# One 512-column matmul for the high weights: a change to the feed-forward loops of an fp32 block kernel on Trainium2

## What is computed

```python
# first block, layers 0 and 1 (conv0, conv1)
up = depthwise_conv(h @ ffn_w_up[l], ffn_conv_w[l], ffn_conv_b[l])     # three taps over the tokens
f = (jax.nn.silu(up[..., :D_FF]) * up[..., D_FF:]) @ ffn_w_down[l]
h = layer_norm(DEEPNORM_ALPHA * h + f, ln_ffn_g[l], ln_ffn_b[l])

# second block, twice per layer (ffn1.0, ffn2.0, ffn1.1, ffn2.1)
def swiglu(h, wi, wo):
    gate, up = jnp.split(h @ wi, 2, axis=-1)
    return (jax.nn.silu(gate) * up) @ wo
x = x + FFN_RESIDUAL * swiglu(rms_norm_2(x, ffn1_norm[i]), ffn1_wi[i], ffn1_wo[i])
```

## Time and profile before

| | |
|---|---|
| median of 3 runs | 1837.57 us (1837.57 to 1838.91) |
| span of the profiled execution, first to last instruction | 1835.9 us |
| busy: PE, PEld | 1797.0 us (98%), 1646.0 us (90%) |
| busy: DVE, ACT, POOL | 1242.9 us (68%), 898.3 us (49%), 94.9 us (5%) |
| mean granted clock of TensorE | 0.999 |
| matmuls | 12420 |

### The profile page before, as it was taken

The page is one execution under the profiler, slowest core; times in us unless marked ns, Lnnn a source line. Parts: engine busy times, 40 slices in busy tenths (PEclk is TensorE's granted clock), DMA queues, the critical chain, the costliest instruction groups (busy, mean ns, idle before and its releaser), DMA issues.

```text
span 1835.9 us, 31204 instructions
## 1 busy us (share of the span) xinstructions
PE 1797.0 (98%) x12420; PEld 1646.0 (90%) x12433; DVE 1242.9 (68%) x1557; ACT 898.3 (49%) x1093; POOL 94.9 (5%) x88
## 2 busy tenths in 40 slices
PE   6999999999999999999999999999999999999999
PEld 6977999897899989999988989999999987889998
DVE  6889876798977686555776655555655577556555
ACT  5566544446644444334645454333533367654332
POOL 1001200000300000000070000000000000000000
PEclk9999999999999999999999999999999999999999
DMA  9525755453574537554633635555555541425553
GB/s 326 182 93 177 260 173 194 160 159 104 179 258 173 206 122 240 185 186 154 189 115 124 243 115 170 190 189 183 174 186 186 192 144 59 172 92 188 187 188 123
DMA packets 232259, 318.55 MB, mean 174 GB/s; under 512 B 12150, under 2 KB 202518, under 8 KB 231670
## 3 DMA queue, kind: packets, MB, share of 16 engines
q1 hardware_dynamic: 226598, 295.97, 48.4%
q0 software_dynamic: 5296, 19.83, 3.4%
q10 hardware_dynamic: 288, 1.69, 0.2%
HBM read 313.27 MB, written 4.19 MB: 173 GB/s over the span
## 4 chain that ended last, share of the span: by engine, by line
PE 91%; DVE 4%; ACT 3%; issue 1%; DMA 0%; ACTq 0%; DVEq 0%
PE bank L708 49%; PE bank L983 19%; PE bank L876 7%; PE bank L731 4%; PE bank L717 3%; PE bank L765 1%; ACT w_hi L1610 1%; DVE w_lo L2242 1%; PE bank L1025 1%; PE bank L1049 1%; DVE x L2239 1%; PE bank L1168 0%; DVE bn L2342 0%; PE bank L1350 0%; PE bank L1364 0%
## 5 line engine op out<-in xcount | busy, mean ns | idle before, releaser
L2242 DVE TENSOR_TENSOR w_lo<-raw,w_hi 128x2048 fp32r<-128x2048 f32 (+2 forms) x279 | 641.6, 2308 | 302.5 <-ACT w_hi L1610 302.0
L1610 ACT ACTIVATE w_hi<-raw 128x2048 fp32r<-128x2048 f32 (+1 forms) x278 | 528.8, 1904 | 633.1 <-PE bank L708 407.9
L708 PE MATMUL bank<-xt_hi,w_hi 128*128 128x256 f32 x2552 | 724.5, 284 | 2.4 <-ACT rb L1610 2.4
L708 PE MATMUL bank<-xt_lo,w_hi 128*128 128x256 f32 x2552 | 722.0, 283 | 0.0
L708 PE MATMUL bank<-xt_hi,w_lo 128*128 128x256 f32 x2552 | 722.0, 283 | 0.0
L708 PEld LDWEIGHTS bank<-xt_hi,w_hi 128*128 128x128 f32 x2552 | 488.3, 191 | 6.6 <-issue 4.0
L708 PEld LDWEIGHTS bank<-xt_lo,w_hi 128*128 128x128 f32 x2552 | 488.3, 191 | 2.6 <-issue 0.2
L708 PEld LDWEIGHTS bank<-xt_hi,w_lo 128*128 128x128 f32 x2552 | 488.3, 191 | 0.2
L983 PE MATMUL bank<-w_hi,act_hi 128*128 128x512 f32 x528 | 206.5, 391 | 0.0
L983 PE MATMUL bank<-w_lo,act_hi 128*128 128x512 f32 x528 | 206.2, 390 | 0.0
L983 PE MATMUL bank<-w_hi,act_lo 128*128 128x512 f32 x528 | 205.4, 389 | 0.0
(11 more groups left out here) (339 smaller groups left out, 1951.9 us busy)
## 6 DMA issues: line engine op xcount, KB each, us to landing
raw<-in_ffn_wi SPq DMA_DIRECT2D x88, 1024.0 KB, 5.1
raw<-in_ffn_w_up SPq DMA_DIRECT2D x44, 1024.0 KB, 5.1
raw<-in_ffn_wo SPq DMA_DIRECT2D x44, 1024.0 KB, 4.9
raw<-in_ffn_w_down SPq DMA_DIRECT2D x22, 1024.0 KB, 5.4
raw<-in_w_in SPq DMA_DIRECT2D x14, 1024.0 KB, 5.6
raw<-in_ssd_in_proj SPq DMA_DIRECT2D x14, 1024.0 KB, 5.3
raw<-in_w_out SPq DMA_DIRECT2D x8, 1024.0 KB, 4.9
raw<-in_even_out_proj SPq DMA_DIRECT2D x8, 1024.0 KB, 5.0
```

The source lines that it names most:

```text
L708: ins = first(mm(dst, w[s][:, k, c0:c0 + m], xt[v][:, k, :], start=k == 0 and p == 0, stop=k == KT - 1 and p == 2))
L1610: return act.activation(dst, src, ACT.Copy)
L2242: return dve.tensor_tensor(out=out, in0=in0, in1=in1, op=op)
```

## The change

The high and low halves of the stream are laid side by side: `xt_both[P, KT, 2, T]`, with `xt_hi` and `xt_lo` as views of it. In the loops of all six feed-forward parts a new helper `tile_halves` makes one output tile into a bank of its own: per slice one 256-column matmul, low weights by high stream, into the left half of the bank, and one 512-column matmul, high weights by both streams, into the whole bank. The left half then holds high by high plus low by high, the right half high by low. Chunks 0 and the down projections are as before.

ScalarE copies the right half of each bank to SBUF (`copy_halves`, into `f_low`); VectorE adds it to the left half (`add_halves`), which frees the bank. Gate takes banks 0 and 1, up banks 2 and 3, in every chunk. Scaling, taps and the product read the sums in SBUF; the taps read `f_sum`.

In the convolution loop the order on both engines is another: the split of a weight unit stands between the sum of gate and its taps, and the split of the third unit stands ahead of the center and taps of up, where it stood behind the operand.

```diff
-        xt_hi = sb("xt_hi", [P, KT, T], F32R)
-        xt_lo = sb("xt_lo", [P, KT, T], F32R)
+        xt_both = sb("xt_both", [P, KT, 2, T], F32R)
+        xt_hi, xt_lo = xt_both[:, :, 0, :], xt_both[:, :, 1, :]
...
+        f_low = carve("ffn", 2, 2, T, at=FFN_TOP)
+        f_sum = carve("ffn", 2, 2, T, at=FFN_TOP + 1024)
...
+                def tile_halves(b, w, j, first):
+
+                    for k in range(KT):
+                        first(mm(bank[b][:, 0:T], w[1][:, k, P * j:P * j + P], xt_hi[:, k, :], start=k == 0, stop=False,
+                                 skip_group_check=True))
+                        ins = mm(bank[b][:, :], w[0][:, k, P * j:P * j + P],
+                                 xt_both[:, k, :, :].rearrange("p v t -> p (v t)"), start=False,
+                                 stop=k == KT - 1, skip_group_check=True)
+                    ins.then_inc(bank_full[b], 1)
...
-                        for b, kk in ((c % 2, k), (2 + c % 2, k + 1)):
-                            pe.wait_ge(bank_drained[b], base[b] + i)
-                            up_pair(kk, b, i)
+                        for b0, kk in ((0, k), (2, k + 1)):
+                            w, first = split_unit(kk, i, KT), First()
+                            for j in range(2):
+                                pe.wait_ge(bank_drained[b0 + j], i * 2 + base[b0 + j] + c - 1)
+                                tile_halves(b0 + j, w, j, first)
...
+            def copy_halves(tag, what, c, turn):
+
+                for j in range(2):
+                    b, n = names.of[f"{tag}.{what}{c}.{j}"]
+                    act.wait_ge(bank_full[b], turn * 2 + n)
+                    copy(f_low[:, "gu".index(what), j, :], bank[b][:, T:2 * T]).then_inc(half_copied, 1)
...
                 with act.Fori(0, TURNS, 1) as i:
+                    seen.enter(i, [(halves_summed, 4), (gate_scaled, 2)])
                     for c in (1, 2):
                         split_in_loop(tag, 3 * c + 1, i)
+                        copy_halves(tag, "g", c, i)
                         split_in_loop(tag, 3 * c + 2, i)
-                        chunk(c, i)
+                        sum_center(c, "g", f_gate, 0, i)
+                        copy_halves(tag, "u", c, i)
+                        split_in_loop(tag, 3 * c + 3, i)
+                        sum_center(c, "u", f_up, 22, i)
+                        act.wait_ge(gate_scaled, seen.next(gate_scaled))
+                        silu(c)
...
+            def add_halves(tag, dst, what, c, turn):
+
+                for j in range(2):
+                    b, n = names.of[f"{tag}.{what}{c}.{j}"]
+                    dve.wait_ge(half_copied, seen.next(half_copied))
+                    ins = tt_(dst[:, j, :], bank[b][:, 0:T], f_low[:, "gu".index(what), j, :], ALU.add)
+                    ins.then_inc(bank_drained[b], 1)
...
                     for c in (1, 2):
                         split_in_loop(tag, 3 * c + 1, i)
+                        sums(c, "g", i)
                         split_in_loop(tag, 3 * c + 2, i)
-                        chunk(c, i)
+                        taps(c, f_sum[:, 0, :, :], f_gate, 0, i).then_inc(gate_scaled, 1)
+                        sums(c, "u", i)
+                        split_in_loop(tag, 3 * c + 3, i)
+                        step(taps(c, f_sum[:, 1, :, :], f_up, 22, i))
+                        product(c)
```

More of the change, by code:

```diff
@@ L1802, in center, with sum_center, silu @@
                         at = bass.ds(44 + t, 1) if turn is None else bass.ds(turn * 4 + 44 + t, 1)
-                        ins = act.activation(dst[:, c % 2, j, :], bank[b][:, T * j:T * j + T], ACT.Identity,
+                        ins = act.activation(dst[:, c % 2, j, :], src[:, j, :], ACT.Identity,
                                              scale=par[:, cw, at], bias=par[:, cb, at])
                     ins.then_inc(center_ready, 1)
[L1807 to L1814, removed]
+                def sum_center(c, what, dst, tile0, turn):
+                    act.wait_ge(halves_summed, seen.next(halves_summed))
+                    center(c, f_sum[:, "gu".index(what), :, :], dst, tile0, turn)
+                def silu(c):
                     act.activation(f_silu[:, c % 2, :], f_gate[:, c % 2, :, :], ACT.Silu).then_inc(silu_ready, 1)
@@ L2535, in ffn @@
                 taken(f"{tag}.rb")
-                gate(0, None)
-                chunk(0, None)
+                first_gate()
+                first_product()
                 with dve.Fori(0, TURNS, 1) as i:
-                    seen.enter(i, [(vec_step, 2), (silu_ready, 2)])
+                    seen.enter(i, [(vec_step, 4), (silu_ready, 2), (half_copied, 8)])
                     for c in (1, 2):
@@ L2562, in taps, with sums, product @@
                             part = dst[:, c % 2, j, 1:T] if side == 0 else dst[:, c % 2, j, 0:T - 1]
-                            src = bank[b][:, T * j:T * j + T - 1] if side == 0 else bank[b][:, T * j + 1:T * j + T]
-                            ins = stt(part, src, w, part, ALU.mult, ALU.add)
+                            ins = stt(part, src[:, j, 0:T - 1] if side == 0 else src[:, j, 1:T], w, part, ALU.mult,
+                                      ALU.add)
                         if side == 0:
                             step(ins)
-                    ins.then_inc(bank_drained[b], 1)
-                def chunk(c, turn):
-                    taps(c, f"{tag}.g{c}", f_gate, 0, turn)
-                    taps(c, f"{tag}.u{c}", f_up, 22, turn)
-                    b, n = names.of[f"{tag}.u{c}"]
-                    dve.wait_ge(bank_drained[b], n if turn is None else turn + n)
+                    return ins
+                def sums(c, what, turn):
+                    add_halves(tag, f_sum[:, "gu".index(what), :, :], what, c, turn)
+                    halves_added(tag, what, c, turn)
+                    dve.sem_inc(halves_summed, 1)
+                def product(c):
                     dve.wait_ge(silu_ready, seen.next(silu_ready))
```

83 lines of the change are left out of this document (52 added, 31 removed).

## The result

The changed kernel takes **1844.6 us** in the median of four runs (1843.45 to 1847.85), the kernel before 1837.6 us. The ratio is 1.0039 with a 95% interval of 1.0027 to 1.005: the change makes the kernel slower by about 7 us. The forecast was 1830.4 us, and the range ended at 1841. It was wrong in sign.

The account below looks back on a forecast made before the run. TensorE's instruction spacing was taken to bound the loops, VectorE and ScalarE mattering only at loop ends. Merge -22.8, entries +9.6, exits +6.0 gave -7.2 us: forecast 1830.4 us, range 1823 to 1841, against 1837.57 before.

Parts of the forecast that it names:

- Term 1, the merge: Up-projection matmuls in the loops: each of 1920 merges saves 11.9 ns, -22.8 us, between -15.6 and -25.6.
- The lower bound of 8.1 ns: Smallest saving per merge in the loops, if every wide matmul took 231.7 ns like the first six: -15.6 us.
- The forecast's own signs: Trace signs against the forecast: a TensorE wait inside a steady chunk, narrow matmuls at 213 ns, or wide ones over 232 ns.
- the first rival: Loop matmuls: the merge saves 0, so the kernel takes 1853 us; decides if wide ones exceed 231.9 ns; chance 0.11.
- the 1848 us by it: Whole-kernel time if a merge in the loops saves only the skill page's 2.5 ns, -4.8 us in all.
- What ScalarE and VectorE get inside a loop: Copies and additions per convolution chunk: ScalarE 9.7, VectorE 14.8 of 16.6 us; both fit, nothing charged.
- The rival of a late VectorE: Convolution loops: hand-over waits exceed VectorE's 1.8 us to spare; at 1 us too much +12, 1842 us; chance 0.07.
- Term 2, entries: Loop entries: TensorE waits for bank 0 to be emptied by VectorE, +9.6 us, bounds +7 and +11.
- Term 3, exits: Two convolution loop exits: the last down unit waits for its operand, 3.0 us each, +6.0 us, between +5 and +7.
- The clock: New gaps in ffn1.0 and at two exits drop TensorE to 1.2 GHz, 1.4 us each, +4.3: 1834.7 us; chance 0.10.
- the added 15.6 us: Forecast cost at the loop ends: entries +9.6 us and convolution exits +6.0 us.
- The fixed 12 ns does not go: Loop matmuls: the width-independent 12 ns stays, the merge saves 0, +15.6 us, 1853 us; chance 0.11.

Follow-up runs that it names:

- 1: Changed kernel with eight wide matmuls, then eight narrow ones per tile, in place of one and one: 1836.4 us, ratio 0.999.
- 6: Changed kernel with two wide and two narrow matmuls in turn: 1835.6 us, ratio 0.9985.
- 7: Changed kernel with eight wide then eight narrow, loop banks exchanged within a pair, and third split behind the operand: 1824.9 us, ratio 0.9924.
- 10: Changed kernel with two wide and two narrow in turn, loop banks exchanged within a pair, and third split behind the operand: 1824.8 us, ratio 0.9922.
- 12: Changed kernel with runs of sixteen of a kind and exchanged banks, the third split left ahead of the taps: 1820.8 us, ratio 0.9911.
- experiment 2: Changed kernel without its merge, three 256-column matmuls per slice again, all else kept: 1857.9 us, ratio 1.0108.
- 8: Changed kernel with runs of sixteen (second tile narrow first), exchanged banks and third split behind the operand: 1822.6 us, ratio 0.9918.
- Experiment 3: Changed kernel with the two banks of each pair exchanged in the loops: 1834.6 us, ratio 0.9978.
- 9: Changed kernel with the wide matmul ahead of its narrow one, still one and one: 1848.2 us, ratio 1.0052.
- 11: Changed kernel with the narrow matmul adding into the right half of the bank: 1845.0 us, ratio 1.0041.
- 13: Changed kernel with the narrow matmul working four slices ahead: 1844.3 us, ratio 1.0038.
- 14: Changed kernel with the narrow matmul taking the high weights too, so the low by high pass is left out: 1847.2 us, ratio 1.0044.

## Why the prediction was wrong

**Term 1, the merge: this step failed.** It took the mean spacing of two pure series, 119.9 and 227.9 ns, for an alternation that no row showed, and got 11.9 ns for a merge. In strict alternation a pair takes 353.1 ns, so a merge brings 359.7 - 353.1 = 6.6 ns; 1920 of them are -12.7 us in place of -22.8. Down then starts slower (5.49 for 5.47), which leaves the -11.4 of the chunks. The lower bound of 8.1 ns failed too: it took the first six wide ones of the earlier trace rows, 231.7 ns, for the worst that a wide one behind narrow ones can be; each of them but one stood behind another wide one. The two switches in the earlier trace rows were read as free at a resolution of 10 ns, where the size in dispute was 4 ns in each wide one. Experiments 1, 6, 7, 10 and 12 show that the forecast's number was right for the instructions (347.8 to 348.3 ns) and wrong only for their order. The forecast's own signs said the same: the wide ones exceed 232 ns, and also the 231.9 at which the first rival decides. Of the 13.7 us between the forecast -7.2 and the measured +6.5 of the span, this term is 11.4, the clock 2.9, and entries and exits give back 0.6.

On the Trainium skill (TensorE: Matmul & The Clock Gate, "Back-to-back issue gap"): its isolated spacing of 215.8 ns for 512 columns was met in no series here; the lowest is 226. Its saving of 2.5 ns per merge is further from the measured 6.6 than my lower bound was. That the 1848 us by it lie closer to 1844.6 than my 1830.4 do is in part luck: its term 1 is -4.8 where the chunks gave -11.4, and the clock, which it left out as well, took back not quite half of that difference.

**What ScalarE and VectorE get inside a loop: right.** VectorE 14.7 us forecast as 14.8, ScalarE 9.6 as 9.7, no wait inside, and experiment 2 gives a chunk of 16.98 to the digit. The rival of a late VectorE did not come true in the changed kernel. It did in a small way where the matmuls were grouped, the banks exchanged and the split stood last (experiments 7, 8 and 10); with the split ahead of the taps it was gone (12).

**Term 2, entries: right in place and in size.** By the starts +9.2 us against +9.6: ffn1.0 +2.65 (forecast 2.7), the other three +0.65 each (0.7), the convolution entries +2.3 each (2.4 and 2.3). Experiment 3 shows that the exchange of two bank numbers buys it all back.

**Term 3, exits: right.** 2.9 us each, forecast 3.0.

**The clock: a rival that came in on top.** It had a chance of 0.10 as a case of its own, but it is a consequence of terms 2 and 3, not another case than the forecast: whoever expects gaps of 3 us should have put their clock price into the sum. Two of the three expected gaps were followed by a stretch at 1.2 GHz in the profiled run, at 1.4 and 1.5 us (expected 1.4 each), and filling the gaps gave back 3.9 us. Which gaps are followed changes from run to run, and the shorter ones of the convolution entries count too (last section). That fits the 1 to 4 us between kernels with the same chunks and the same waits (9, 11, 13 and 14).

**The fixed 12 ns does not go:** half true. It said that a saving of 8.1 ns breaks even with the added 15.6 us; the saving was 6.6, and the slower start of down and the clock made the rest. It was given 0.11 and priced as all or nothing; the truth lay between it and the forecast, where I had put no weight.

What stays open: why single narrow and wide matmuls in turn cost 5 ns a pair. Excluded are the order in the pair (9), the bank's half (11), the slice of the stream (13), the weight array (14) and a fixed price per change of width (6). Whether the weight loads or the matmuls themselves hold the pace was not separated by any run. The alternation by single instructions is left, as a fact without a mechanism.

## What to carry to other kernels

A spacing read in a pure series is not the spacing in a mixture: when the forecast hangs on a few ns per instruction, demand a row with the same order, or give the sign no better than even odds. Where matmuls of two widths are mixed, try them in groups of two or more; here, with 256 and 512 columns of fp32, that gave 8 to 9 us. At a loop's entry, look which bank the first tile takes; where an added 3 us gap on TensorE was followed by the lower clock, it cost about half as much again here. Read gaps from start to start, since a list of waits depends on which records are there.

## What the runs showed of the hardware

**Single alternation.** 353.1 ns a pair of 256 and 512 columns in turn, 348.3 ns in groups of two or eight, 347.8 in groups of sixteen; the narrow one takes 117 ns in single alternation, 115 in groups of two and 119 in groups of eight; the wide one 236, 233 (in groups of two), 230 (in groups of eight) or 226 when settled.

**The clock behind short gaps.** In the profiled runs of the changed kernel and its variants, a stretch at a granted clock of 0.50 stands behind every wait of 3.2 us at the entry of ffn1.0 that was left empty (nine of nine), behind 13 of 20 waits of 2.9 us at the convolution exits, and behind 8 of 20 waits of 2.0 us at the convolution entries.

**VectorE and GpSimd take turns.** The slow split of the earlier trace rows, which set the size of the convolution entries, has its cause in the trace of the changed kernel at conv0 (start us, us, engine, line, operation):

```profile
181.28 2.41 POOL L3202 TENSOR_TENSOR x<-mix,wide 128x1024 f32<-128x1024 f32 x1 [24.64 <-DVE w_lo L2277]
...
181.81 4.03 DVE L2277 TENSOR_TENSOR w_lo<-raw,w_hi 128x2048 fp32r<-128x2048 f32 x1 [0.70 <-ACT w_hi L1628]
...
183.77 4.28 POOL L3203 TENSOR_TENSOR x<-x,wide 128x1024 f32<-128x1024 f32 x1
...
188.13 2.41 POOL L3202 TENSOR_TENSOR x<-mix,wide 128x1024 f32<-128x1024 f32 x1
...
189.26 1.83 DVE L2277 TENSOR_TENSOR work<-work 128x512 f32<-128x512 f32 x1
```

The split's record begins at 181.81, and GpSimd's ends at 183.69; 2.29 us from there, the split's usual time, is 185.98, and it ended at 185.84. GpSimd's next one, 4.28 us long on record, ends 2.2 us behind the split's end. The product takes 1.83 in place of 0.69 beside the third. The Trainium skill (SBUF — State Buffer, "SBUF: two separate sides") says that the two engines share one port pair which one of them holds for a whole instruction, two SBUF inputs on VectorE being one of the cases; these rows agree. That moving GpSimd's work away would shorten the entries was not tried.
